# Seven products of the last feed-forward block: one more PSUM bank for each group, the evictions of two corners joined, six banks in turn instead of four

## The chip, the cores and the metric

The kernel runs on one core of a Trainium2 chip (trn2). The metric is the device time of one execution in microseconds (us), as the median of several runs. The core's engines run side by side and meet only at semaphores: TensorE (PE) multiplies and adds up in PSUM, which has eight banks of 512 float32 per partition; VectorE (DVE) and ScalarE (ACT) read PSUM and work in SBUF; SyncE (SP) issues the transfers. Each engine works through its own list of instructions in order, so an instruction that waits holds back all that stand behind it on that engine.

## The reference

The reference is one inference step of a decoder trunk with two layers, in float32. Each layer has a token mixer (an mLSTM in the first, gated linear attention in the second) and then a dense SwiGLU feed-forward, each between two RMS norms and added to x:

```
def swiglu(x, w_gate, w_up, w_down):
    h = jax.nn.silu(einsum('bsd,df->bsf', x, w_gate)) * einsum('bsd,df->bsf', x, w_up)
    return einsum('bsf,fd->bsd', h, w_down)

for i in range(DEPTH):
    mix, state = mixer_i(rms_norm(x, g_pre_mix[i]), ...)
    x = x + rms_norm(mix, g_post_mix[i])
    x = x + rms_norm(swiglu(rms_norm(x, g_pre_ffn[i]), w_ffn_gate[i], w_ffn_up[i], w_ffn_down[i]), g_post_ffn[i])
```

There are 1024 prompt tokens and 64 sample tokens, the model is 1024 wide, the feed-forward 2816 wide (22 tiles of 128).

## The kernel before

**Units.** The 1088 tokens are worked in block 0 (512 tokens) and block 1 (576 tokens, as two halves of 288 since a PSUM bank takes 512). `Plan` (from L118) writes a list of units, one per weight tile of 128x1024: P (input projection), W (output projection), G (gate), U (up), D (down; four output tiles for a pair of hidden tiles). Every engine's program walks this list. A float32 weight tile is split in a high part (`w_hi`, ACT, L1618) and a low part (`w_lo`, DVE, L2061), and each product is three matmuls: low x high, high x high, high x low. Weight tiles live in rings of three: `hi(n)` waits until unit n-3 has finished its matmuls (semaphore `groups`), `lo(n)` waits for `hi(n)`, and the transfer of a tile waits for `lo` of three units before.

**Seven products.** In block 1 of the second layer's feed-forward, the last large stage of the kernel, 18 groups (9 of gate, 9 of up, in turn) compute two neighbouring tiles at once. Two tiles x two halves of the contraction x two halves of the tokens would be eight products of 12 matmuls; with sums of weights (S1, S2, S4) and of inputs (T0 to T3) it is seven. A group is two units, first and second. In TensorE's order (`seven_first`, L1255; `seven_second`, L1276) with banks X, Y, Z:

1. product 1 into X; 2. product 2 (S2) into Y; 3. product 3 (S1) into Z; 4. product 4 added to Y;
5. product 5 added to X, which is corner c11; 6. product 6 (second tile x T3) into Y anew; 7. product 7 (S4) added to Z.

ScalarE copies X after product 1 (L1648, `first_copy`). VectorE forms U2 = Y + copy after product 2, U3 = Y + copy after product 4, c22 = Z + U3 at once, then c21 = Y + U3 after product 6 and c12 = Z + U2 after product 7 (all L2105). Product 6 waits for U3, since it overwrites Y, and product 7 waits for c22, since it adds to Z. For a gate group ScalarE then puts c11 through silu (L1654, `first_silu`, which waits for product 5), splits a weight tile (`hi`, L1618), and puts c21 and c22 together through silu (L1659); c12 follows (L1664). For an up group VectorE multiplies c11 (L2129) and in `gate` the three others (L2145) with the gate's values.

**Order on VectorE.** In the second unit of a gate group it is: U3, c22, `lo(n + 2)`, c21; then, in eight of the gate groups, a piece of block 0's last norm (`post`, L2340 and L2343). In the D unit that follows it is c12, the weight sums of the next group (`s3_s2`, L2084 and L2087), and the evictions Y of the four down tiles (L2202), with splits between them.

**Banks.** `Plan.banks` hands out banks 0 to 3 in turn; block 1's tiles take two at a time, so in a D unit tile q waits until tile q-2 (or what was there before) is evicted. Banks 4 to 7 (`M0` = 4) belong to mixers and norms; in this stage the norm of block 0 uses banks 4 and 5.

**Start of the stage.** The sums T0 to T3 are formed on VectorE (`tsum`) and split (`tq`, L1703 and L2236) while the last down units of block 0 (D, L2297) run. The order of the units is G0, D, D, U0, G1, U1, then the first group of seven. G, U with a number are hidden tiles of block 1 that are computed in the ordinary way.

Of the kernel before, what the change touches and what calls it, by code (L numbers as in the profile page):

```python
# [13 lines left out]
P = 128  # L14
# [94 lines left out]
class Plan:  # L109
# [61 lines left out]
    def banks(self):  # L171
        at, n = 0, 0
        counts = {"act": 0, "dve": 0}
        held = [None] * 4
        for u in self.units:
            if u.seven:
                z = u.seven
                if not u.second:
                    z.banks = [(at + c) % 4 for c in range(3)]
                    z.vacated = [dict([held[b]]) for b in z.banks]  # L180
                    at = (at + 3) % 4
                    z.t1 = counts["act"] = counts["act"] + 1
                    z.u2 = counts["dve"] = counts["dve"] + 1
                else:
                    order = ("u3", "c22", "c21", "c12") if z.kind == "G" else ("u3", "c22", "c11", "c21", "c12")
                    if z.kind == "G":
                        z.c11 = counts["act"] = counts["act"] + 1
                    ev = {}
                    for name in order:
                        counts["dve"] += 1  # L190
                        ev[name] = counts["dve"]
                    z.u3, z.c22, z.c21, z.c12 = ev["u3"], ev["c22"], ev["c21"], ev["c12"]
# [3 lines left out]
                    held[z.banks[1]] = ("dve", z.c21)  # L196
                    held[z.banks[2]] = ("dve", z.c12)
                u.groups.append(Group(n, z.banks[u.second], {}, 0))
                n += 1
                continue  # L200
            by = "dve" if u.kind in "UD" or u.late else "act"
            if u.part is not None:
                if u.part == 0:
                    mine = [Group(0, (at + c) % 4, {held[(at + c) % 4][0]: held[(at + c) % 4][1]}, 0) for c in range(4)]
                if u.part < 3:
                    u.groups.append(Group(n, None, {}, 0))
                    n += 1
                for c, grp in enumerate(mine if u.part == 3 else ()):
                    counts[by] += 1
                    grp.n, grp.ev = n, counts[by]  # L210
                    held[grp.bank] = (by, grp.ev)
                    u.groups.append(grp)
                    n += 1
                u.chunks = mine
                continue
            for _ in range(4 if u.kind == "D" else 1):
                if u.blk and at % 2:
                    at = (at + 1) % 4
                mine = range(at, at + NG[u.blk])
# [5 lines left out]
                u.groups.append(Group(n, at, vacated, counts[by]))  # L225
                for b in mine:
                    held[b] = (by, counts[by])
                at = (at + NG[u.blk]) % 4
                n += 1
# [10 lines left out]
def schedule(plan):  # L240
# [254 lines left out]
def memory(nc, ctx):  # L495
# [31 lines left out]
    g.E = sb("evicted", [P, 3, NT[1]])  # L527
    g.C = sb("state", [P, H, DV + 1])
# [45 lines left out]
    g.UC = piece("n", "up_corner", [P, GW[1]])  # L574
# [68 lines left out]
def program(nc, g, plan, a):  # L643
# [114 lines left out]
    n_gated = 0  # L758
    for n, u in enumerate(units):
        if u.seven and not u.second:  # L760
            sevens[n] = u.seven
            u.seven.n, u.seven.hid0, u.seven.gated0 = n, u.hid0, n_gated
            n_gated += 3 * (u.kind == "U")
# [22 lines left out]
    n = 0  # L786
# [29 lines left out]
    with nc.Block() as block:  # L816
# [288 lines left out]
        def _(pe):  # L1105
# [149 lines left out]
            def seven_first(z):  # L1255

                a, b = z.n % NW, (z.n + 1) % NW
                X, Y, Z = z.banks
# [3 lines left out]
                half_product(g.whi[:, a, 0:512], g.wlo[:, a, 0:512], quarter(HH, 0, 0), quarter(HL, 0, 0), X).then_inc(s["prod"], 1)  # L1262
# [6 lines left out]
                vacant(z.vacated[2])  # L1269
# [6 lines left out]
            def seven_second(z):  # L1276

                a, b = z.n % NW, (z.n + 1) % NW
                X, Y, Z = z.banks
                HH, HL = g.HH[1], g.HL[1]  # L1280
                pe.wait_ge(s["left_act"], z.t1)
# [318 lines left out]
        def _(act):  # L1600
# [26 lines left out]
            def s2_s1_high(z):  # L1627
                act.wait_ge(s["sums"], 4 * z.g + 2)
                wait(act, s["prod"], 5 * (z.g - 1) + 2)
                act.activation(g.S2H[:, :], g.SF[:, :], ACT.Copy).then_inc(s["s_hi"], 1)  # L1630
                act.wait_ge(s["sums"], 4 * z.g + 3)
                wait(act, s["prod"], 5 * (z.g - 1) + 3)
                act.activation(g.S1H[:, :], g.S1[:, :], ACT.Copy).then_inc(s["s_hi"], 1)

            def s4_high(z):
                act.wait_ge(s["sums"], 4 * z.g + 4)
                wait(act, s["prod"], 5 * z.g)
                act.activation(g.S4H[:, :], g.SF[:, :], ACT.Copy).then_inc(s["s_hi"], 1)

            def first_copy(z):  # L1640

                act.wait_ge(s["prod"], 5 * z.g + 1)
                act.wait_ge(s["hid_lo_ready"], z.hid0 - 2 * (z.kind == "G" and z.g > 0))
                if z.kind == "U":
                    act.wait_ge(s["left_dve"], z.mate.c21)
                elif z.g:
                    act.wait_ge(s["gated"], z.gated0 - 1)
# [9 lines left out]
            def second_silu(z):  # L1657
                act.wait_ge(s["left_dve"], z.c21)
# [8 lines left out]
            def hid_high(z):  # L1667
                for j, c in enumerate((1, 0)):
                    act.wait_ge(s["left_dve"], z.c11)
                    act.wait_ge(s["gated"], z.gated0 + 2 + j)  # L1670
                    act.activation(g.hh[:, c, :], g.E[:, c, :], ACT.Copy).then_inc(s["hid_hi_ready"], 1)

            def seven_unit(n, u):

                z, before, after = u.seven, ended(n), sevens.get(n + 1)
                if not u.second:
# [3 lines left out]
                    if before:  # L1680
                        hid_high(before)
# [8 lines left out]
                hi(n + 2)  # L1690

            def between(n):

                before = ended(n)
                if before:
                    third_silu(before) if before.kind == "G" else hid_high(before)
# [8 lines left out]
            def evict(u):  # L1705
# [46 lines left out]
                elif u.kind == "G":  # L1752
# [6 lines left out]
                    if u.i < 2:  # L1759
                        wait(act, s["hid_lo_ready"], u.hid0 - u.i)  # L1760
# [267 lines left out]
            for n, u in enumerate(units):  # L2028
# [16 lines left out]
                evict(u)  # L2045
                if n + 1 in sevens:
                    s2_s1_high(sevens[n + 1])
                for t in u.tags:
# [4 lines left out]
        def _(dve):  # L2053
# [35 lines left out]
            def s1_sum(z):  # L2089
                summed(z, 2)  # L2090
                wait(dve, s["prod"], 5 * (z.g - 1) + 3)
# [15 lines left out]
            def u2_sum(z):  # L2107
                dve.wait_ge(s["prod"], 5 * z.g + 2)
# [7 lines left out]
            def u3_c22(z):  # L2116
                dve.wait_ge(s["prod"], 5 * z.g + 4)
                add_to(U3(), z.banks[1], U3())
                dve.wait_ge(s["left_dve"], z.u3)
# [3 lines left out]
                add_to(g.E[:, 1, GW[1]:] if z.kind == "G" else g.UC[:, :], z.banks[2], U3())  # L2123
# [7 lines left out]
            def c21(z):  # L2131
                dve.wait_ge(s["groups"], units[z.n + 1].groups[0].n + 1)
                add_to(g.E[:, 1, 0:GW[1]] if z.kind == "G" else U3(), z.banks[1], U3())

            def c12(z):
                dve.wait_ge(s["prod"], 5 * z.g + 5)
                add_to(g.E[:, 0, GW[1]:] if z.kind == "G" else U2(), z.banks[2], U2())

            def gate(z):

                for E, up, silu, left in ((g.E[:, 1, GW[1]:], g.UC[:, :], 1, z.c22), (g.E[:, 1, 0:GW[1]], U3(), 1, z.c21),
                                          (g.E[:, 0, GW[1]:], U2(), 2, z.c12)):
                    dve.wait_ge(s["silu"], z.mate.g + silu)
                    dve.wait_ge(s["left_dve"], left)
                    dve.tensor_tensor(E, up, E, ALU.mult).then_inc(s["gated"], 1)  # L2145
# [8 lines left out]
            def seven_first(n, z, before):  # L2154

                if before:
                    c12(before)
                    if before.kind == "U":
                        gate(before)
# [10 lines left out]
            def seven_second(n, z, after):  # L2170
# [628 lines left out]
            for n, u in enumerate(units):  # L2799
# [15 lines left out]
                if before:  # L2815
                    c12(before)
                    gate(before)
# [18 lines left out]
                seven_ahead(n)  # L2836
# [101 lines left out]
```

## Time and profile before

| | |
|---|---|
| median of 3 runs | 2555.53 us (2555.3 to 2555.64) |
| the profiled execution's own time | 2555.54 us |
| its span in the trace | 2553.5 us |
| granted TensorE clock, mean | 0.999 |
| PE busy | 2533.4 us (99%) |
| DVE busy | 1622.4 us (64%) |
| ACT busy | 1056.4 us (41%) |
| stage of the seven products | about 2156 to 2482 us of the span, a period of 35.8 us |

A period is one gate group, two D units and one up group: 84 + 96 + 84 = 264 matmuls. A matmul's recorded duration (about 295 ns) is longer than the distance to the next one (about 132 ns), because they overlap; so a wait of TensorE is read from the starts of its weight loads (PEld), which come one per matmul. Times below are microseconds from the span's start.

### The profile page before, as it was taken

What the parts mean: (1) busy time and instruction counts of PE and PEld (TensorE: products, weight loads), DVE (VectorE), ACT (ScalarE), POOL (GpSimd) and SP (SyncE); (2) the same over time, 40 slices, a digit from 0 to 9 for tenths busy, and PEclk for the clock granted to TensorE, in tenths of its full rate; (3) what the DMA queues carried; (4) which work ended last, traced back from release to release, by engine and by line L of the source; (5) the groups of instructions that cost most, each with busy time, mean ns of one, the idle gap of its engine ahead of it and who ended that gap; (6) DMA issues with size and microseconds to landing.
All of it is one profiled execution on the core that took longest, in us unless ns stands there. A gap on an engine that the chain in (4) does not pass through costs nothing.

```text
span 2553.5 us, 40896 instructions
## 1 busy us (share of the span) xinstructions
PE 2533.4 (99%) x16985; PEld 2287.3 (90%) x16985; DVE 1622.4 (64%) x2562; ACT 1056.4 (41%) x1537; POOL 0.2 (0%) x4
## 2 busy tenths in 40 slices
PE   9999999999999999999999999999999999999998
PEld 7899898887988998889998988998887988999998
DVE  6743575566467673357754776327877388888875
ACT  5443355442334442444524344326453345333332
POOL 0000000000000000000000000000000000000000
PEclk9999999999999999999999999999999999999999
DMA  6454445435433433543323343344436333333332
GB/s 227 136 181 154 144 152 158 143 113 167 153 114 106 137 103 97 164 156 99 110 94 126 96 146 111 134 146 135 133 89 215 121 128 105 102 97 91 104 97 93
DMA packets 176707, 330.40 MB, mean 129 GB/s; under 512 B 19964, under 2 KB 93436, under 8 KB 176524
## 3 DMA queue, kind: packets, MB, share of 16 engines
q1 hardware_dynamic: 176524, 327.79, 40.4%
q8 instruction: 135, 2.21, 0.4%
q14 instruction: 48, 0.39, 0.0%
HBM read 271.46 MB, written 56.28 MB: 128 GB/s over the span
## 4 chain that ended last, share of the span: by engine, by line
PE 89%; DVE 6%; ACT 2%; issue 1%; DMA 1%; SPq 0%; DVEq 0%; ACTq 0%
PE ps L1118 71%; PE ps L1246 6%; PE ps L1132 3%; PE ps L1496 1%; DVE w_lo L2061 1%; ACT w_hi L1618 1%; PE ps L1438 1%; PE ps L1582 1%; DVE Y L2297 1%; PE ps L1427 1%; PE ps L1421 1%; DVE Y L2340 0%; PE ps L1300 0%; PE ps L1150 0%; PE ps L1420 0%
## 5 line engine op out<-in xcount | busy, mean ns | idle before, releaser
L1118 PE MATMUL ps<-HH,w_lo 128*128 128x288 f32 (+1 forms) x2904 | 968.4, 333 | 1.7 <-DVE Y L2297 1.6
L1118 PE MATMUL ps<-HL,w_hi 128*128 128x288 f32 (+1 forms) x2904 | 958.3, 330 | 0.0
L1118 PE MATMUL ps<-HH,w_hi 128*128 128x288 f32 (+1 forms) x2904 | 957.8, 330 | 0.0
L2061 DVE TENSOR_TENSOR w_lo<-w_stage,w_hi 128x1024 fp32r<-128x1024 f32 x392 | 478.3, 1220 | 231.8 <-ACT w_hi L1618 230.7
L1118 PEld LDWEIGHTS ps<-HH,w_lo 128*128 128x128 f32 x2904 | 544.9, 188 | 50.7 <-issue 6.0
L1118 PEld LDWEIGHTS ps<-HL,w_hi 128*128 128x128 f32 x2904 | 544.9, 188 | 43.0
L1118 PEld LDWEIGHTS ps<-HH,w_hi 128*128 128x128 f32 x2904 | 545.0, 188 | 41.6
L1618 ACT ACTIVATE w_hi<-w_stage 128x1024 fp32r<-128x1024 f32 x392 | 412.4, 1052 | 316.7 <-PE ps L1118 268.9
L1118 PE MATMUL ps<-hid_hi,w_lo 128*128 128x288 f32 (+1 forms) x1052 | 349.7, 332 | 5.3 <-DVE Y L2297 2.1
L1118 PE MATMUL ps<-hid_lo,w_hi 128*128 128x288 f32 (+1 forms) x1052 | 343.6, 327 | 0.0
L1118 PE MATMUL ps<-hid_hi,w_hi 128*128 128x288 f32 (+1 forms) x1052 | 343.4, 326 | 0.0
L2297 DVE TENSOR_TENSOR Y<-ps,Y 128x512 f32<-128x512 f32 (+1 forms) x255 | 178.5, 710 | 74.5 <-PE ps L1118 74.3
L1118 PEld LDWEIGHTS ps<-hid_hi,w_lo 128*128 128x128 f32 x1052 | 197.4, 188 | 28.4 <-issue 4.0
L1118 PEld LDWEIGHTS ps<-hid_lo,w_hi 128*128 128x128 f32 x1052 | 197.5, 188 | 14.0
L1118 PEld LDWEIGHTS ps<-hid_hi,w_hi 128*128 128x128 f32 x1052 | 197.5, 188 | 13.1
L1769 ACT ACTIVATE hid_hi<-evicted 128x512 fp32r<-128x512 f32 (+1 forms) x70 | 45.6, 651 | 256.3 <-DVE evicted L2279 256.3
L2072 DVE TENSOR_TENSOR n_sum<-n_sum,n_sq 128x512 f32<-128x512 f32 (+1 forms) x110 | 79.4, 721 | 92.7 <-ACT n_sq L1624 88.9
L1736 ACT ACTIVATE evicted<-ps 128x576 f32<-128x576 f32 (+1 forms) x64 | 40.8, 637 | 211.9 <-PE ps L1118 211.8
L2279 DVE TENSOR_TENSOR evicted<-ps,evicted 128x512 f32<-128x512 f32 (+1 forms) x70 | 49.9, 712 | 78.6 <-PE ps L1118 78.5
L1765 ACT ACTIVATE evicted<-ps 128x512 f32<-128x512 f32 (+1 forms) x70 | 43.1, 616 | 98.7 <-PE ps L1118 98.0
L2282 DVE TENSOR_TENSOR hid_lo<-evicted,hid_hi 128x512 fp32r<-128x512 f32 (+1 forms) x70 | 50.2, 717 | 50.2 <-ACT hid_hi L1769 50.2
L1624 ACT ACTIVATE n_sq<-n_xs 128x512 f32<-128x512 f32 (+1 forms) x64 | 41.7, 657 | 91.3 <-DVE n_xs L2343 84.4
(323 smaller groups left out, 2899.4 us busy)
## 6 DMA issues: line engine op xcount, KB each, us to landing
w_stage<-w_gate_in SPq DMA_DIRECT2D x88, 512.0 KB, 3.7
w_stage<-w_up_in SPq DMA_DIRECT2D x88, 512.0 KB, 3.6
w_stage<-w_down_in SPq DMA_DIRECT2D x88, 512.0 KB, 3.6
w_stage<-w_in_in SPq DMA_DIRECT2D x80, 512.0 KB, 3.8
w_stage<-w_out_in SPq DMA_DIRECT2D x32, 512.0 KB, 3.6
proj_scratch<-evicted SPq DMA_DIRECT2D x48, 288.0 KB, 2.2
proj_scratch<-evicted SPq DMA_DIRECT2D x32, 256.0 KB, 2.1
w_stage<-w_v_in SPq DMA_DIRECT2D x16, 512.0 KB, 4.1
```

What stands on the lines that cost most here:

```text
L1118: mm = pe.matmul(ps[:, grp.bank + t, 0:W], wsl(w, k), x[:, k, t * W:(t + 1) * W], start=(k == first and m == 0), stop=(k == last and m == 2))
L1132: mm = pe.matmul(ps[:, grp.bank, :], x[:, k, t], w[:, n % NW, cols], start=(k == 0 and m == 0), stop=(k == KD - 1 and m == 2))
L1246: mm = pe.matmul(ps[:, bank, 0:GW[1]], w[:, k * P:(k + 1) * P], x[:, k, :], start=start and k == 0 and m == 0, stop=k == KD // 2 - 1 and m ...
L1618: act.activation(g.whi[:, n % NW, :], g.wst[:, n % NW, :], ACT.Copy).then_inc(s["w_hi"], 1)
L1624: act.activation(grouped(dst, b) if src.shape != dst.shape else dst, src, ACT.Square).then_inc(s["squared"], 1)
L1765: act.activation(grouped(g.E[:, c, 0:NT[b]], b), bank(grp.bank, b), ACT.Silu).then_inc(s["left_act"], 1)
L1769: act.activation(g.hh[:, u.i % 2, 0:NT[b]], g.E[:, 2, 0:NT[b]], ACT.Copy).then_inc(s["hid_hi_ready"], 1)
L2061: dve.tensor_tensor(g.wlo[:, n % NW, :], g.wst[:, n % NW, :], g.whi[:, n % NW, :].bitcast(F32), ALU.subtract).then_inc(s["w_lo"], 1)
L2072: dve.tensor_tensor(acc, acc, sq, ALU.add).then_inc(s["summed"], 1)
L2279: dve.tensor_tensor(grouped(pr, b), bank(grp.bank, b), grouped(g.E[:, u.i % 2, 0:NT[b]], b), ALU.mult).then_inc(s["left_dve"], 1)
L2282: dve.tensor_tensor(g.hl[:, u.i % 2, 0:NT[b]], pr, g.hh[:, u.i % 2, 0:NT[b]].bitcast(F32), ALU.subtract).then_inc(s["hid_lo_ready"], 1)
L2297: dve.tensor_tensor(Y, bank(grp.bank, b), Y, ALU.add).then_inc(s["left_dve"], 1)
```

## The change

It does five things.

- In the last stage (from the first G of block 1 in layer 2) the banks in turn are six: 0, 1, 2, 3, 6, 7.
- A group of seven takes four of them: X, Y, W, Z, with W and Z side by side. Product 6 goes to W, starts anew there, and stands ahead of product 5. It no longer waits for U3, and its number is the fifth.
- VectorE forms c21 and c22 in one instruction of 576 columns, `c2`, from banks W and Z; product 7 waits for it, in place of c22. `c2` waits for product 6. In a gate group it stands behind `lo(n + 2)`; in an up group behind S2's split and S4's sum of the next group.
- `gate` is two instructions: c21 and c22 together, right behind `c2`, then c12. `hid_high` of that half moves to the second unit.
- At the start of the stage the order is G0, G1, D, D, U0, U1; `tq` 2 and 3, the load of x for block 0's norm (`xload` 8) and the weight sums ahead of the first group stand earlier.

```diff
-        self.puts(A1[49:-2] + B1[:1] + A1[-2:] + B1[1:])
+        self.puts(A1[49:-2] + B1[0:3:2] + A1[-2:] + B1[1:4:2] + B1[4:])
@@ Plan.banks
+            if u.layer == 1 and u.blk == 1 and u.kind == "G":
+                pool = (0, 1, 2, 3, 6, 7)
+            size = len(pool)
-                    z.banks = [(at + c) % 4 for c in range(3)]
+                    at = (at + at % 2) % size
+                    z.banks = [pool[(at + c) % size] for c in range(4)]
-                    order = ("u3", "c22", "c21", "c12") if z.kind == "G" else ("u3", "c22", "c11", "c21", "c12")
+                    order = ("u3", "c2", "c12") if z.kind == "G" else ("u3", "c2", "c11", "c12")
@@ schedule
-        tag(f + (0, 0, 3, 4)[i], "tq", i)
-    tag(f + 5, "xload", 8)
+        tag(f + i // 2, "tq", i)
+    tag(f + 3, "xload", 8)
@@ TensorE, seven_second
+                vacant(z.vacated[2])
+                half_product(g.whi[:, b, 512:1024], g.wlo[:, b, 512:1024], g.TH[:, 3], g.TL[:, 3], W
+                             ).then_inc(s["prod"], 1)
                 pe.wait_ge(s["left_act"], z.t1)
                 half_product(g.whi[:, a, 512:1024], g.wlo[:, a, 512:1024], quarter(HH, 1, 0), quarter(HL, 1, 0), X, False
-                             ).then_inc(s["groups"], 1)
-                pe.wait_ge(s["left_dve"], z.u3)
-                half_product(g.whi[:, b, 512:1024], g.wlo[:, b, 512:1024], g.TH[:, 3], g.TL[:, 3], Y
-                             ).then_inc(s["groups"], 1)
+                             ).then_inc(s["groups"], 2)
                 pe.wait_ge(s["s_lo"], 3 * z.g + 3)
-                pe.wait_ge(s["left_dve"], z.c22)
+                pe.wait_ge(s["left_dve"], z.c2)
                 half_product(g.S4H, g.S4L, quarter(HH, 1, 1), quarter(HL, 1, 1), Z, False).then_inc(s["prod"], 1)
@@ ScalarE, seven_unit (second unit; unchanged but for its last line)
                 if z.kind == "G":
                     first_silu(u)
                     hi(n + 2)
                     second_silu(z)
                     return
                 if after:
                     s2_s1_high(after)
                 hi(n + 2)
+                hid_high(z, 0)
@@ VectorE
+            def c2(z):
+                dve.wait_ge(s["prod"], 6 * z.g + 5)
+                dve.wait_ge(s["left_dve"], z.u3)
...
+                out = grouped(g.E[:, 1, :], 1) if z.kind == "G" else g.UC[:, :, :]
+                dve.tensor_tensor(out, bank(z.banks[2], 1), U3().unsqueeze(1).to_broadcast([P, 2, GW[1]]), ALU.add
+                                  ).then_inc(s["left_dve"], 1)
@@ VectorE, seven_second
-                u3_c22(z)
+                u3_sum(z)
+                if z.kind == "G":
+                    lo(n + 2)
+                    c2(z)
+                    return
                 if after:
                     s_low(after, 0)
-                if z.kind == "G":
-                    lo(n + 2)
-                    c21(z)
-                    return
+                    s4_sum(after)
+                c2(z)
+                gate(z, 0)
                 c11_product(z)
                 if after:
-                    s4_sum(after)
                     s_low(after, 1)
-                c21(z)
                 lo(n + 2)
@@ VectorE, main loop: the weight sums ahead of a group
                 if u.kind != "D" and n + 2 < len(units):
                     lo(n + 2)
+                seven_ahead(n)
...
-                seven_ahead(n)
```

## Rows read from the trace of the kernel before

**Rows 1.** The page: busy time of each engine, its share of the span, and instructions.
```profile
PE 2533.4 (99%) x16985; PEld 2287.3 (90%) x16985; DVE 1622.4 (64%) x2562; ACT 1056.4 (41%) x1537; POOL 0.2 (0%) x4
```

**Rows 2.** The chain of waits in time: start us, us, what; the groups of two periods.
```profile
2220.91 19.13 PE ps L1246 x144
...
2256.67 19.13 PE ps L1246 x144
```

**Rows 3.** Timeline of weight loads: start us, us, engine line op [idle before <-releaser].
```profile
2239.73 0.19 PEld L1246 LDWEIGHTS ps<-t_hi,w_lo 128*128 128x128 f32 x1
...
2241.32 0.19 PEld L1246 LDWEIGHTS ps<-HH,n_s_lo 128*128 128x128 f32 x1
...
2244.85 0.19 PEld L1118 LDWEIGHTS ps<-hid_hi,w_lo 128*128 128x128 f32 x1 [0.27 <-DVE evicted L2105]
...
2246.84 0.19 PEld L1118 LDWEIGHTS ps<-hid_hi,w_lo 128*128 128x128 f32 x1 [0.37 <-DVE Y L2202]
```

**Rows 4.** Who waited for whom, 2195 to 2475: us in total, times, longest.
```profile
DVE w_lo L2061 <- ACT w_hi L1618: 16.2, 8, 2.0
...
PEld ps L1118 <- DVE Y L2202: 3.0, 8, 0.4
PEld ps L1118 <- DVE evicted L2105: 2.2, 8, 0.3
```

**Rows 5.** Timeline of ScalarE, second unit of a gate group.
```profile
2240.06 0.41 ACT L1654 ACTIVATE evicted<-ps 128x288 f32<-128x288 f32 x1 [4.83 <-PE ps L1246]
2240.36 1.05 ACT L1618 ACTIVATE w_hi<-w_stage 128x1024 fp32r<-128x1024 f32 x1
```

**Rows 6.** Timeline of VectorE, the same gate group and the D units behind it.
```profile
2241.45 1.23 DVE L2061 TENSOR_TENSOR w_lo<-w_stage,w_hi 128x1024 fp32r<-128x1024 f32 x1 [2.02 <-ACT w_hi L1618]
2242.59 0.45 DVE L2105 TENSOR_TENSOR evicted<-ps,evicted 128x288 f32<-128x288 f32 x1
2242.96 0.74 DVE L2340 SCALAR_TENSOR_TENSOR Y<-Y,vec,n_rstd 128x512 f32<-128x512 f32 x1
...
2251.93 0.76 DVE L2202 TENSOR_TENSOR Y<-ps,Y 128x576 f32<-128x576 f32 x1 [0.24 <-PE ps L1118]
```

**Rows 7.** Timeline of VectorE, then of weight loads, second unit of an up group.
```profile
2227.55 0.45 DVE L2105 TENSOR_TENSOR evicted<-ps,evicted 128x288 f32<-128x288 f32 x1
2228.03 0.46 DVE L2105 TENSOR_TENSOR n_up_corner<-ps,evicted 128x288 f32<-128x288 f32 x1
2228.41 0.68 DVE L2102 TENSOR_TENSOR s_lo<-n_s_s,s_hi 128x512 fp32r<-128x512 f32 x1
...
2230.16 0.19 PEld L1246 LDWEIGHTS ps<-HH,n_s_lo 128*128 128x128 f32 x1
```

**Rows 8.** Start of the stage, timeline of weight loads: those that had waited.
```profile
2129.46 0.19 PEld L1118 LDWEIGHTS ps<-hid_hi,w_lo 128*128 128x128 f32 x1 [1.39 <-issue]
...
2137.06 0.19 PEld L1118 LDWEIGHTS ps<-HH,w_lo 128*128 128x128 f32 x1 [1.96 <-DVE w_lo L2061]
...
2160.74 0.19 PEld L1246 LDWEIGHTS ps<-t_hi,s_lo 128*128 128x128 f32 x1 [2.53 <-DVE s_lo L2102]
...
2175.32 0.19 PEld L1118 LDWEIGHTS ps<-hid_hi,w_lo 128*128 128x128 f32 x1 [1.45 <-DVE Y L2200]
```

**Rows 9.** The same stretch: busy us (instructions) of PE, PEld, DVE, ACT; then timelines.
```profile
2130.00:2160.00 30.00, 26.85 (x181) 24.93 (x179) 24.44 (x33) 17.52 (x23) 0.00 (x0) 1.00 0.18 54
...
2163.49 0.46 DVE L2105 TENSOR_TENSOR evicted<-ps,evicted 128x288 f32<-128x288 f32 x1 [0.62 <-ACT evicted L1648]
...
2149.88 1.28 ACT L1765 ACT_TABLE_LOAD   x1
```

**Rows 10.** TensorE's last matmuls; windows: length, PE busy, granted clock, DMA share, GB/s.
```profile
2541.78 4.04 PE L1352 MATMUL ps<-Y,ident 128*128 128x288 f32 x16
...
2548.00:2548.50 0.50, 0.00 (x0) 0.94 0.98 378
2548.50:2549.00 0.50, 0.00 (x0) 0.50 1.00 373
```

More of the change, by code:

```diff
@@ L178, in banks @@
                 if not u.second:
-                    z.banks = [(at + c) % 4 for c in range(3)]
-                    z.vacated = [dict([held[b]]) for b in z.banks]
-                    at = (at + 3) % 4
+                    at = (at + at % 2) % size
+                    z.banks = [pool[(at + c) % size] for c in range(4)]
+                    z.vacated = [dict([held[b]] if held[b] else []) for b in z.banks]
+                    at = (at + 4) % size
                     z.t1 = counts["act"] = counts["act"] + 1
@@ L191, in banks @@
                         ev[name] = counts["dve"]
-                    z.u3, z.c22, z.c21, z.c12 = ev["u3"], ev["c22"], ev["c21"], ev["c12"]
+                    z.u3, z.c2, z.c12 = ev["u3"], ev["c2"], ev["c12"]
                     if z.kind == "U":
@@ L195, in banks @@
                     held[z.banks[0]] = ("act" if z.kind == "G" else "dve", z.c11)
-                    held[z.banks[1]] = ("dve", z.c21)
-                    held[z.banks[2]] = ("dve", z.c12)
+                    held[z.banks[1]] = ("dve", z.u3)
+                    held[z.banks[2]] = ("dve", z.c2)
+                    held[z.banks[3]] = ("dve", z.c12)
                 u.groups.append(Group(n, z.banks[u.second], {}, 0))
@@ L217, in banks @@
                 if u.blk and at % 2:
-                    at = (at + 1) % 4
-                mine = range(at, at + NG[u.blk])
+                    at = (at + 1) % size
+                mine = range(pool[at], pool[at] + NG[u.blk])
                 vacated = {}
@@ L224, in banks @@
                 counts[by] += 1
-                u.groups.append(Group(n, at, vacated, counts[by]))
+                u.groups.append(Group(n, pool[at], vacated, counts[by]))
                 for b in mine:
                     held[b] = (by, counts[by])
-                at = (at + NG[u.blk]) % 4
+                at = (at + NG[u.blk]) % size
                 n += 1
@@ L762, in program @@
             u.seven.n, u.seven.hid0, u.seven.gated0 = n, u.hid0, n_gated
-            n_gated += 3 * (u.kind == "U")
+            u.seven.before = last_seven
+            last_seven = u.seven
+            n_gated += 2 * (u.kind == "U")
     def ended(n):
@@ L1257, in seven_first @@
                 a, b = z.n % NW, (z.n + 1) % NW
-                X, Y, Z = z.banks
+                X, Y, W, Z = z.banks
                 HH, HL = g.HH[1], g.HL[1]
@@ L1636, in s4_high @@
                 act.wait_ge(s["sums"], 4 * z.g + 4)
-                wait(act, s["prod"], 5 * z.g)
+                wait(act, s["prod"], 6 * z.g)
                 act.activation(g.S4H[:, :], g.SF[:, :], ACT.Copy).then_inc(s["s_hi"], 1)
             def first_copy(z):
-                act.wait_ge(s["prod"], 5 * z.g + 1)
+                act.wait_ge(s["prod"], 6 * z.g + 1)
                 act.wait_ge(s["hid_lo_ready"], z.hid0 - 2 * (z.kind == "G" and z.g > 0))
[L1644 to L1647, printed above, removed]
+                if z.before:
+                    act.wait_ge(s["left_dve"], z.before.c2)
                 act.activation(U3(), ps[:, z.banks[0], 0:GW[1]], ACT.Copy).then_inc(s["left_act"], 1)
@@ L1680, in seven_unit @@
                     if before:
-                        hid_high(before)
+                        hid_high(before, 1)
                     return
@@ L1695, in between @@
                 if before:
-                    third_silu(before) if before.kind == "G" else hid_high(before)
+                    third_silu(before) if before.kind == "G" else hid_high(before, 1)
             def t_half(i):
@@ L1759, in evict @@
                     if u.i < 2:
-                        wait(act, s["hid_lo_ready"], u.hid0 - u.i)
+                        wait(act, s["hid_lo_ready"], u.hid0 - (u.i if units[n - 1].kind == "U" else 0))
                     elif unit("U", u.layer, b, u.i - 2).seven:
@@ L2090, in s1_sum @@
                 summed(z, 2)
-                wait(dve, s["prod"], 5 * (z.g - 1) + 3)
+                wait(dve, s["prod"], 6 * (z.g - 1) + 3)
                 dve.tensor_tensor(g.S1[:, :], g.SF[:, :], stage(z.n, 0), ALU.add).then_inc(s["sums"], 1)
@@ L2129, in c11_product, with gate @@
                 dve.tensor_tensor(E, ps[:, z.banks[0], 0:GW[1]], E, ALU.mult).then_inc(s["left_dve"], 1)
-            def c21(z):
-                dve.wait_ge(s["groups"], units[z.n + 1].groups[0].n + 1)
-                add_to(g.E[:, 1, 0:GW[1]] if z.kind == "G" else U3(), z.banks[1], U3())
             def c12(z):
[L2136 to L2145, printed above, removed]
+                dve.wait_ge(s["prod"], 6 * z.g + 6)
+                add_to(g.E[:, 0, GW[1]:] if z.kind == "G" else U2(), z.banks[3], U2())
+            def gate(z, j):
+                dve.wait_ge(s["silu"], z.mate.g + 1 + j)
+                dve.wait_ge(s["left_dve"], z.c12 if j else z.c2)
+                if j:
+                    dve.tensor_tensor(g.E[:, 0, GW[1]:], U2(), g.E[:, 0, GW[1]:], ALU.mult).then_inc(s["gated"], 1)
+                else:
+                    dve.tensor_tensor(grouped(g.E[:, 1, :], 1), g.UC[:, :, :], grouped(g.E[:, 1, :], 1), ALU.mult
+                                      ).then_inc(s["gated"], 1)
             def hid_low(z, j):
@@ L2158, in seven_first @@
                     if before.kind == "U":
-                        gate(before)
+                        gate(before, 1)
                 s_low(z, 2)
@@ L2816, in _ @@
                     c12(before)
-                    gate(before)
+                    gate(before, 1)
                     hid_low(before, 0)
```

39 lines of the change are left out of this document (20 added, 19 removed).

## Prediction

> **What bounds the kernel now.** I read the page first: TensorE is busy 99% of the span, VectorE 64%, ScalarE 41% [rows 1]. So time goes or comes only where TensorE's row of matmuls opens or closes. Then the chain of waits in time, which shows how regular the last stage is: from one pair of groups to the next it is 2256.67 - 2220.91 = 35.76 us [rows 2]. Then the weight loads one by one, as matmul records overlap: the twelve of product 6 take 2241.32 - 2239.73 = 1.59 us, 0.1325 each [rows 3], and 264 of them 34.98 us. The rest of a period, 0.78 us, is two waits in the D unit behind the gate group. A load lasts 0.19 and loads come 0.13 apart, so a wait costs TensorE the idle time shown plus 0.06: 0.27 + 0.06 = 0.33 for the bank that c12 still holds, and 0.37 + 0.06 = 0.43 for the first down tile's eviction [rows 3]; each is there eight times [rows 4]. At the start of the stage there are larger ones (matmuls of 512 columns come 0.23 apart, so there the idle time counts less 0.04): 1.35 and 1.92 in and behind block 0's last D units, 2.59 before product 2 of the first group, 1.51 in the first D unit of block 1 [rows 8]. All that more banks could win in this stage is thus 8 x 0.76 + 7.4 = 13.5 us, 0.5% of the time. (0.2%, 5.1 us, is about what a measurement of this kernel can tell from no change.)
>
> **Gate groups: a new wait ahead of product 7.** This decides the sign. Before, c22 was read ahead of `lo`, so product 7 was free long before its turn. Now product 7 waits for `c2`, and on VectorE `c2` stands behind `lo(n + 2)`. That waits for `hi(n + 2)` on ScalarE, which stands behind `first_silu`; both wait for product 5, the one right ahead of product 7 in TensorE's order. So TensorE finishes product 5 and then sits through a whole chain over ScalarE and VectorE. VectorE's wait is in the trace already, with no harm yet: it idles 2.02 us before `lo`, eight times, 16.2 us [rows 4, 6]. The links, from the end of product 5, whose successor's first load starts at 2239.73:
> - to the silu: 2240.06 - 2239.73 = 0.33 [rows 3, 5];
> - silu to `hi`: 2240.36 - 2240.06 = 0.30 [rows 5];
> - `hi` to `lo`: 2241.45 - 2240.36 = 1.09 [rows 5, 6];
> - `lo` to the next VectorE instruction: 2242.59 - 2241.45 = 1.14 [rows 6];
> - `c2` itself: the trace has no sum from two banks with one operand read twice. The nearest row is the addition of 576 columns out of PSUM, 0.76 [rows 6]; below it is one corner, 0.45, and above two corners, 0.92 [rows 6, 7]. I take 0.76;
> - from VectorE to TensorE 0.05: the weight load of 2246.84 follows an eviction at about that distance.
>
> Sum 3.67 us, between 3.4 and 3.8, in each of nine gate groups: +33.0 us. Behind the waiting product 7 on TensorE stand the D units and all that follows; nothing covers it. In the first group the silu table has to be loaded too: the norm's exp comes after G1 now, so the load of 1.28 us that G1's silu paid [rows 9] falls to `first_silu`: +1.3.
>
> **D units: both waits go, -6.1 us.** With six banks a down tile waits for the one three before it, 4.8 us away. c12 sits in bank 3, which only the third tile takes. The piece of the norm, which starts at 2242.96 [rows 6] and made the first eviction late, now runs while TensorE waits for nothing else than `c2`; it stands behind `c2`, so it doesn't lengthen the wait. 8 x 0.76 = 6.1. The first D unit's 1.51 was VectorE waiting for a weight tile that landed late; the load of x that shared the DMA engines with it is now issued earlier, and the longer group covers the rest: -1.5.
>
> **Up groups: nothing.** VectorE's order is U3, split of S2, sum S4, `c2`. From 2227.55: U3 0.38, split and sum at most 0.68 each, so `c2` starts by 2229.3 and ends by 2230.05, plus 0.05. Product 7's turn is 2230.16 [rows 7]. Product 6, for which `c2` waits, ends at 2228.57 + 0.3. I take 0, for 0.1 us of slack; if it is late by a whole split, 0.6 in each of nine, +5. It can't gain, since nothing waited here. Fewer instructions on VectorE (one for two corners, two for three in `gate`) save about 0.3 a period where it idles anyway: 0.
>
> **Start of the stage: nothing.** G1's 48 matmuls now cover the splits of T, and the down tiles have six banks, so 1.35 and 1.92 at block 0's D units go. But VectorE is the one that is late here: it is busy 24.44 of 30 us [rows 9], its work stays the same, and two more splits of T (1.3 each) come ahead of the first down eviction. Carrying its list forward in the new order (D's evictions and norm sums from about 2133.6 for 12 us, the norm's reciprocal root, U0, U1, the sums for the first group), I get U2 of the first group at about 2163.5, where it is now: 2163.49 [rows 9]. TensorE waits in other places (rstd, product 2, product 4) for the same sum. I take 0; at best all three go, 1.35 + 1.92 + 2.59 = 5.9 gained; at worst 2 lost.
>
> **The clock.** It is granted at 1.00, that is 2.4 GHz, over the stage. It fell to 0.50 (1.2 GHz) once in this trace, close to 2548.0 to 2548.5, about 2.6 us after TensorE's last matmul ended at 2545.82 [rows 10]; the idle stretch of 2.53 before product 2 [rows 8] did not bring it down. The new wait leaves TensorE idle for about 3.5 us, longer than both. No row here shows matmuls at the lower level. At half the clock a product takes 1.59 more, so a fall costs about that, with 0 and 9 falls as the ends: 0 to 14.3. I take two falls, +3.2.
>
> The Trainium skill (TensorE: Matmul & The Clock Gate, section "HAM oscillation — how this bites in real kernels") says that gaps between bursts of matmuls can send the clock down again and again, each burst starting cold. By it all nine waits would pay, and the sum would be 11 us higher; the second rival is that. This trace shows one fall, after the last matmul, which agrees, and none in a shorter gap.
>
> **Sum.** Against the profiled execution's own 2555.54 (span 2553.5 and 2.0 around it; the median of the runs is 2555.53, so no shift): + 33.0 + 1.3 - 6.1 - 1.5 + 3.2 = +29.9, 2585.4; I say 2585 us.
>
> **Rivals.**
> 1. The waits in the D units stay: they would be VectorE's lateness and not the banks'. The second wait's releaser is an eviction that stood behind the norm piece. Against it: VectorE gets that piece done in the new wait. 2585 + 7.6 = 2593.
> 2. The clock falls in every gate group and stays down for one to two products: 2585 - 3.2 + 14.3 = 2596, up to 2610. For it: the idle time is longer than that after which it fell; against: only one such case.
> 3. The start gains in full: 2585 - 5.9 = 2579. For it: banks were waited for there; against: VectorE's 24.44 of 30.
> 4. The other side, faster: product 7 does not wait for `lo`. If the high part of that tile were ready before product 5 ends, `c2` would be done in time and only the gains stay: 2555.5 - 6.1 - 1.5 = 2548. It decides at the moment when `hi` starts: before the end of product 5 or behind it. For it speaks only that `c2`'s other inputs are early; against it, that ScalarE's `hi` starts 0.30 behind a silu that waits for product 5 [rows 5], in all eight periods [rows 4].
> 5. The change doesn't do what it says, by halves: the down units still take banks that groups hold. Product 7's wait is as computed, the gain 3 less: 2588, inside the forecast.
>
> **How the numbers follow.** Forecast (with 5) 0.66, own range 2575 to 2594; rival 1 0.08; rival 2 0.12; rival 3 0.08; rival 4 0.06. Low: the start's gain and no fall of the clock, 2579 - 3.2, less 3 for a shorter `c2`: 2573. High: 2600, which takes in rival 1 and the lower part of rival 2. Faster 0.06, within 0.2% 0.02, slower 0.92.
>
> **What would show it.** In the timeline of weight loads each gate group has a gap of about 3.7 us before product 7, released by a VectorE addition of 576 columns of some 0.76; the chain of waits shows L1618 and L2061 in each period; the period is 35.76 - 0.76 + 3.67 = 38.7 us. VectorE's idle time before `lo` in the gate group becomes some 4.0 (2.02, one product of 1.59, and c22's 0.4), with `c2` right behind. No load in the D units waits. The granted clock in windows of a few us shows the falls. It would be wrong if product 7 of the gate groups follows product 5 without a gap, if up groups wait too, or if the start of the stage moves product 1 of the first group by more than 3 us against product 4.

## The result: 1.45% slower, as forecast in sign and cause

| | before | after |
|---|---|---|
| median of four runs | 2555.47 us | 2593.51 us |
| fastest and slowest | 2555.30, 2555.64 | 2590.90, 2594.91 |
| profiled execution | 2555.54 | 2593.95 |
| its span, mean granted clock | 2553.5, 0.999 | 2592.2, 0.993 |

The ratio is 1.0145 (95% interval 1.0133 to 1.0157). The forecast was 2585, with 2573 to 2600 as its range: 8.5 us short. Of the runs in this document three executions stand apart and stay unexplained: one each of experiments 1 and 6 took over 6000 us at clock 1.00 (without them these two medians would be 0.15 and 0.2 lower), and one of experiment 9 took 2549.89 at 0.948. Line numbers of the kernel after are some ten higher (L1618 is now L1628, L2061 is L2070).

**The profile after.** The page's busy times, and the chain that ended last by engine, against [rows 1]:

```profile
PE 2543.1 (98%) x16985; PEld 2301.2 (89%) x16985; DVE 1621.8 (63%) x2535; ACT 1056.1 (41%) x1537; POOL 0.2 (0%) x4
PE 92%; DVE 5%; ACT 2%; issue 2%; DVEq 0%; ACTq 0%
```

VectorE and ScalarE are no busier, and their shares of the chain are no larger either (before it was PE 89%, DVE 6%, ACT 2%). What has changed is where they stand in it. The chain of waits in order of time (start, length, engine, line; "issue" is time without a wait that the profile shows) tells where, in one period, against [rows 2]:

```profile
2228.18 20.71 PE ps L1255 x156
2248.89 0.02 issue
2248.91 0.02 ACT evicted L1662
2248.94 0.28 issue
2249.22 1.06 ACT w_hi L1628
2250.28 0.02 issue
2250.30 0.04 DVE w_lo L2070
2250.34 0.05 issue
2250.38 0.05 DVEq L490
2250.43 1.01 issue
2251.44 0.76 DVE evicted L2137
2252.20 0.14 issue
2252.34 2.70 PE ps L1255 x12
```

This is the predicted chain link by link: product 5 ends, `first_silu` at 2248.91, `hi` at 2249.22, `lo` at 2250.30, `c2` at 2251.44 for 0.76, and product 7. The waits grouped by who waits for whom (total, times, longest), first TensorE's from 2150 to 2525 us:

```profile
PE ps L1255 <- DVE evicted L2137: 31.2, 9, 3.5
PE ps L1255 <- DVE s_lo L2111: 2.8, 1, 2.8
PE ps L1255 <- DVE evicted L2114: 1.7, 1, 1.7
```

L2137 is `c2`, nine times. The other two are the start of the stage. No weight load in a D unit waits any more, where there had been sixteen [rows 4]. VectorE's own wait for `hi`, 2195 to 2510 us, was 16.2 in eight [rows 4]:

```profile
DVE w_lo L2070 <- ACT w_hi L1628: 32.9, 8, 4.1
```

The weight loads of the same group one by one (start, us, tiles, in brackets the idle time ahead of it and its releaser), the last of product 5 and the first of product 7, against [rows 3]:

```profile
2248.46 0.19 PEld L1255 LDWEIGHTS ps<-HL,w_hi 128*128 128x128 f32 x1
2252.31 0.19 PEld L1255 LDWEIGHTS ps<-HH,n_s_lo 128*128 128x128 f32 x1 [3.66 <-issue]
```

From load to load 3.85 us, where 0.13 would be without a wait: 3.72 lost, and so in all nine groups. On VectorE, against [rows 6]:

```profile
2250.30 1.23 DVE L2070 TENSOR_TENSOR w_lo<-w_stage,w_hi 128x1024 fp32r<-128x1024 f32 x1 [4.11 <-ACT w_hi L1628]
2251.44 0.75 DVE L2137 TENSOR_TENSOR evicted<-ps,evicted 128x576 f32<-128x576 f32 x1
2252.11 0.74 DVE L2354 SCALAR_TENSOR_TENSOR Y<-Y,vec,n_rstd 128x512 f32<-128x512 f32 x1
```

The norm piece stands behind `c2` and under the cover of product 7. What the forecast had too small is in the table of stretches (stretch, its length, PE busy with instructions, granted clock, DMA share, GB/s), one stretch a period:

```profile
2168.50:2209.70 41.20, 37.74 (x266) 0.92 0.25 77
2209.70:2248.50 38.80, 35.34 (x267) 1.00 0.30 89
2248.50:2288.70 40.20, 36.74 (x265) 0.96 0.27 86
2288.70:2329.00 40.30, 36.84 (x266) 0.96 0.29 86
2329.00:2370.20 41.20, 37.74 (x267) 0.92 0.28 84
2370.20:2408.90 38.70, 35.24 (x266) 1.00 0.28 89
2408.90:2449.20 40.30, 36.84 (x266) 0.96 0.27 86
2449.20:2489.50 40.30, 36.84 (x267) 0.96 0.29 85
2489.50:2530.70 41.20, 37.74 (x267) 0.92 0.29 84
```

The two periods at 1.00 last 38.75, the forecast's 38.7. Seven are longer: four at 0.96 by 1.5 us, three at 0.92 by 2.45. The same view in small steps around one wait:

```profile
2248.50:2252.70 4.20, 0.74 (x6) 1.00 0.00 0
2252.70:2253.20 0.50, 0.50 (x6) 0.77 0.00 0
2253.20:2256.00 2.80, 2.80 (x13) 0.50 0.47 162
2256.00:2256.50 0.50, 0.50 (x4) 0.61 0.67 238
```

Here the clock holds 1.00 through the idle time, falls to 0.50 (1.2 GHz) as the matmuls resume, and is back at 1.00 from about 2256.4 on. At 0.50 weight loads come 0.24 us apart instead of 0.1325; these two are five apart:

```profile
2254.60 0.33 PEld L1127 LDWEIGHTS ps<-hid_hi,w_lo 128*128 128x128 f32 x1
2255.80 0.33 PEld L1127 LDWEIGHTS ps<-hid_lo,w_hi 128*128 128x128 f32 x1
```

So 1 us of matmuls at 0.50 costs 1 - 0.1325 / 0.24 = 0.45 us, and the 3.4 us from 2253.0 to 2256.4 cost the 1.5 us of this period. In the three periods at 0.92 the clock falls earlier, while TensorE still waits. In the first of them product 7's first load comes at 2172.36, and the granted clock was already

```profile
2171.00:2171.50 0.50, 0.00 (x0) 0.55 0.00 0
```

and 0.50 from there to about 2177.9. That leaves 5.5 us of matmuls at 0.50, which cost the 2.45.

### The profile page after: what moved, and what is told of

It reads as the page before. It is cut to its first block, busy times and chain, and to the rows that moved or that the text cites. A ratio compares the mean times of both kernels' runs of the same rounds, so it can differ in the third digit from the quotient of the medians.

```text
span 2592.2 us, 40859 instructions
## 1 busy us (share of the span) xinstructions
PE 2543.1 (98%) x16985; PEld 2301.2 (89%) x16985; DVE 1621.8 (63%) x2535; ACT 1056.1 (41%) x1537; POOL 0.2 (0%) x4
## 4 chain that ended last, share of the span: by engine, by line
PE 92%; DVE 5%; ACT 2%; issue 2%; DVEq 0%; ACTq 0%
PE ps L1127 71%; PE ps L1255 8%; PE ps L1141 3%; PE ps L1506 1%; ACT w_hi L1628 1%; PE ps L1159 1%; PE ps L1448 1%; PE ps L1592 1%; DVE Y L2311 1%; PE ps L1437 1%; PE ps L1431 1%; PE ps L1310 0%; DVE w_lo L2070 0%; PE ps L1430 0%; PE ps L1539 0%
## 5 line engine op out<-in xcount | busy, mean ns | idle before, releaser
L2070 DVE TENSOR_TENSOR w_lo<-w_stage,w_hi 128x1024 fp32r<-128x1024 f32 x392 | 478.5, 1221 | 249.7 <-ACT w_hi L1628 248.7
L1628 ACT ACTIVATE w_hi<-w_stage 128x1024 fp32r<-128x1024 f32 x392 | 412.1, 1052 | 335.9 <-PE ps L1127 278.4
```

What stands on the lines that cost most here:

```text
L1628: act.activation(g.whi[:, n % NW, :], g.wst[:, n % NW, :], ACT.Copy).then_inc(s["w_hi"], 1)
L2070: dve.tensor_tensor(g.wlo[:, n % NW, :], g.wst[:, n % NW, :], g.whi[:, n % NW, :].bitcast(F32), ALU.subtract).then_inc(s["w_lo"], 1)
```

## The experiments

The "kernel before" was timed again beside each (its median there is given). Theory: product 7 waits because `c2` stands behind `lo(n + 2)`, which waits for a tile whose high part starts only after product 5; the clock adds to it. Rivals: contention for banks, or the order at the start of the stage.

**1. `c2` ahead of `lo`**, nothing else changed.

```diff
                 if z.kind == "G":
-                    lo(n + 2)
                     c2(z)
+                    lo(n + 2)
                     return
```

> The changed kernel with c2 ahead of lo(n + 2) in the gate groups. Theory (VectorE's order makes the wait ahead of product 7, and the clock falls because of it): the nine gaps of 3.72 us go (33.5 us) and the clock stays at 1.00 (13.4 us), so about 2547 us if no wait comes back in the D units. I expect one to come back: lo and the piece of the norm are then late again, the first down tile is evicted until about 0.4 us after the fourth one wants its bank, so 0.4 a period against 0.76 before the change: 2550 us. Rival (the gaps come from the four banks or from c2's width, not from lo): 2590 us or more, gaps stay.

Measured: 2551.16 us against 2556.65, ratio 0.9978 (0.9969 to 0.9987). The gap ahead of product 7 is gone from all nine groups, and the mean clock is 0.999. One line moved takes back the whole 38 us and 5.5 more. The waits of weight loads in 2195 to 2475 us, and one of them:

```profile
PEld ps L1127 <- DVE Y L2216: 2.5, 8, 0.3
```
```profile
2247.24 0.19 PEld L1127 LDWEIGHTS ps<-hid_hi,w_lo 128*128 128x128 f32 x1 [0.31 <-DVE Y L2216]
```

The first D wait (the bank c12 held) stays away, the second is back at 0.31 + 0.06 = 0.37, since `lo` and the norm piece again run late.

**2. The wait filled with matmuls.** To price the clock, the kernel after gets 26 extra matmuls behind product 5 of each gate group, into two banks that nothing reads; their results are not used.

```diff
                              ).then_inc(s["groups"], 2)
+                if z.kind == "G":
+                    for i in range(26):
+                        pe.matmul(ps[:, M0 + i % 2, 0:GW[1]], HH[:, 0, 0:P], g.TH[:, 3, i % 4, :], start=True, stop=True)
```

> The changed kernel with 26 extra matmuls (3.4 us, results unused) behind product 5 of each gate group, where TensorE waits. Theory (7 of 9 waits bring the clock down, which costs 13.4 us beyond the waits): the clock stays at 1.00 in the stage, the load of product 7 starts when it did, 2593.5 - 13.4 = 2580 us. Rival (the 13.4 us are something else in these periods): 2593 us or more.

Measured: 2581.01 us against 2556.65, 1.0096 (1.0082 to 1.0110): 12.5 us less than the kernel after, with 234 matmuls more. The table of stretches, in two that hold all nine groups (their ends are not those of this kernel's periods):

```profile
2168.50:2209.70 41.20, 41.12 (x311) 1.00 0.26 78
2209.70:2530.00 320.30, 319.62 (x2399) 1.00 0.30 92
```

The chain over ScalarE and VectorE is as long as before (in the first group product 7's first load comes 8.48 us behind product 4's, 8.47 in the kernel after), only the clock does not fall in the groups. From the first gate tile's first load to the first load of the last product 7 it is 2507.05 - 2117.03 = 390.02 us here and 2519.62 - 2116.35 = 403.27 in the kernel after: 13.25 less, where the table of the kernel after gives 4 x 1.5 + 3 x 2.45 = 13.4. (The spans differ by 2592.2 - 2579.6 = 12.6, since this execution came to the stage 0.7 later.) So of the 38 us some 13 are the clock's. The other 25 are the waits of 33.5 less what the D units and the start give back.

One fall there is in this trace, ahead of the groups, at the wait before product 2 of the first group, 2.8 us long as in the kernel after, where the clock stayed up:

```profile
2160.00:2162.00 2.00, 2.00 (x11) 0.50 0.26 55
```

It costs nothing: product 4, which waits for VectorE in any case, comes 47.53 us after the first gate tile's first load, and 47.54 in the kernel after.

**3. The kernel before with its corner late**: four banks, three-bank groups, but c22 behind `lo(n + 2)` in gate groups.

```diff
                 add_to(U3(), z.banks[1], U3())
+                if z.kind == "U":
+                    c22(z)
+
+            def c22(z):
                 dve.wait_ge(s["left_dve"], z.u3)
...
                     lo(n + 2)
+                    c22(z)
                     c21(z)
```

> The kernel before with one edit: c22 of the gate groups behind lo(n + 2). Theory (the order on VectorE alone is enough): product 7 waits for the chain less product 6, which still covers 1.6 us: about 1.84 us in each of nine groups; the D units' waits of 0.76 and the first one of 1.5 go in exchange: 2564 us, clock 1.00. Rival (banks, c2 or product order are needed for the loss): 2555.5 us, no gap ahead of product 7.

Measured: 2565.38 us against 2556.65, 1.0035 (1.0021 to 1.0049). TensorE's waits from 2150 to 2530 us, and a first load of the product that waits:

```profile
PE ps L1246 <- DVE evicted L2105: 14.1, 9, 1.6
```
```profile
2245.36 0.19 PEld L1246 LDWEIGHTS ps<-HH,n_s_lo 128*128 128x128 f32 x1 [1.78 <-issue]
```

Nine gaps of 1.97 - 0.13 = 1.84 us, half the length, since product 6 still covers 1.6 us of the chain and c22 alone takes 0.3 less than `c2`; 16.6 us lost, 7.6 won at the D units, whose waits are gone with four banks too: +9.0, measured +8.7. The order on VectorE alone makes the wait, and with TensorE's waits at 1.6 us the clock stays at 1.00.

**4. Experiment 1 with four banks.**

```diff
-                pool = (0, 1, 2, 3, 6, 7)
+                pool = (0, 1, 2, 3)
```

> e1 with four banks in turn instead of six. Theory (with groups of four banks, six in turn are needed): the second down tile waits for c12, about 1.5 us, the third for the first's eviction, 0.5: some 1.6 a period more than e1, 2563 us. Rival (the waits in the D units are VectorE's lateness, whatever the banks): as e1 within 2 us.

Measured: 2564.53 us against 2556.65, 1.0032 (1.0019 to 1.0044). The waits of weight loads, 2195 to 2470 us:

```profile
PEld ps L1127 <- DVE evicted L2114: 12.1, 8, 1.5
PEld ps L1127 <- DVE Y L2216: 2.5, 7, 0.4
```

A group of four banks in a pool of four makes the D unit wait for c12 for 1.5 us instead of the 0.27 of [rows 3]. So the two extra banks are needed for the four-bank group, and are worth 13.4 us to it; that is a price which the change itself brought in.

**5. The start of the stage as before** (experiment 1 with the old unit order and the old places of T's splits and of the load of x; the weight sums stay early).

```diff
-        self.puts(A1[49:-2] + B1[0:3:2] + A1[-2:] + B1[1:4:2] + B1[4:])
+        self.puts(A1[49:-2] + B1[:1] + A1[-2:] + B1[1:])
...
-        tag(f + i // 2, "tq", i)
-    tag(f + 3, "xload", 8)
+        tag(f + (0, 0, 3, 4)[i], "tq", i)
+    tag(f + 5, "xload", 8)
```

> e1 with the old start of the stage: the order G0, D, D, U0, G1, U1, and tq 2, 3 and xload 8 where they were; the early weight sums stay. Theory (VectorE's list bounds the start, so its new order gave nothing; only the earlier load of x takes away the 1.5 in the first D unit): 1.5 to 2 slower than e1, 2553 us. Rival (the new start won the 5.9 of its three waits): 2557 us.

Measured: 2549.17 us against 2556.16, 0.9973 (0.9962 to 0.9984). Both expectations missed: undoing the order made it faster. The measure of the start is the time from the first gate tile's first load to that of product 4 of the first group. The two loads in this kernel:

```profile
2117.62 0.19 PEld L1127 LDWEIGHTS ps<-HH,w_lo 128*128 128x128 f32 x1 [0.60 <-DVE w_lo L2070]
2163.60 0.19 PEld L1255 LDWEIGHTS ps<-t_hi,w_lo 128*128 128x128 f32 x1 [1.95 <-issue]
```

and in the kernel after:

```profile
2116.35 0.19 PEld L1127 LDWEIGHTS ps<-HH,w_lo 128*128 128x128 f32 x1 [0.55 <-DVE w_lo L2070]
2163.89 0.19 PEld L1255 LDWEIGHTS ps<-t_hi,w_lo 128*128 128x128 f32 x1 [1.95 <-issue]
```

That is 47.54 us after (47.54 in experiment 1 too, 47.72 before), and 45.98 here. The near-zero of the start was two parts of opposite sign: the new order, with the places of the splits, costs 1.56, and what else moved there wins 47.72 - 45.98 = 1.74. What is left over is `seven_ahead`, called ahead of the tags, the high parts of these weight sums, which ScalarE now forms ahead of its own evictions, and the six banks. None of them was run alone. Experiment 4 speaks against the banks: with four of them product 4 comes at 2164.68 - 2117.14 = 47.54 us too.

**6. The norm piece between `c2` and `lo`** in gate groups, on top of experiment 1.

```diff
                     c2(z)
+                    for t in units[n].tags:
+                        if t[0] == "post":
+                            post(*t[1:])
                     lo(n + 2)
...
-                        if t[0] in steps:
+                        if t[0] in steps and t[0] != "post":
```

> e1 with the piece of the norm between c2 and lo(n + 2), where VectorE waits for ScalarE anyway. Theory (the wait of 0.37 that e1 has left in each period is the first down tile's eviction, late by the piece of the norm): all eight go, 2551.2 - 3.0 = 2548.2 us. Rival (that eviction is late for the weight sums or lo itself): as e1.

Measured: 2548.21 us against 2556.16, 0.9969 (0.9956 to 0.9981). No weight load waits from 2195 to 2470 us. The second D wait was the norm piece standing ahead of the first eviction; VectorE was idle ahead of `lo` and could take it there.

**7. The reciprocal root of the last norm later**, on top of 6: into the first up group, where it had stood ahead of the first group's U sums.

```diff
-    ffn_norm(3, 0, u + 1, [(at["G", 1, 1, 2 * p + 1, 0] - u - 1, 1) for p in range(2, 10)])
+    v = at["U", 1, 1, 3, 0]
+    ffn_norm(3, 0, v, [(at["G", 1, 1, 2 * p + 1, 0] - v, 1) for p in range(2, 10)])
```

> e6 with the reciprocal root of block 0's norm moved from U0 into the second unit of the first up group of seven. Theory (with VectorE's list the bound at the start, the root's chain over ScalarE and its three instructions are what makes products 2 and 4 of the first group late): of the start's 6.0 us of waits some 3.5 go, 1.5 come back where the root now stands, 2546 us. Rival (the start waits for the splits of T and the weight sums alone): as e6, or 1 to 2 slower.

Measured: 2545.57 us against 2556.16, 0.9958 (0.9945 to 0.9970). Product 4 comes 42.27 us after the first load, 5.3 sooner; where the root stands now, two waits of 0.74 and 1.77 from load to load give 2.3 back. In the kernel after, VectorE's list has the root's three instructions there, and a wait of 1.9 for what ScalarE does for it:

```profile
2154.05 0.69 DVE L2338 SCALAR_TENSOR_TENSOR n_sum<-n_rstd 128x512 f32<-128x512 f32 x1 [1.91 <-ACT n_rstd L1805]
```

The three take 2156.23 - 2154.05 = 2.2 us, so 4.1 of the 5.3 are these, and the rest stands ahead of them, at the root's partial sums. That bears out that VectorE's list, with its waits for ScalarE in it, bounds the start; and the 47.54 of experiment 4 says that it isn't the banks.

**8. `hi` ahead of `first_silu`** in gate groups of the kernel after: the shortest chain with `lo` still ahead of `c2`.

```diff
                 if z.kind == "G":
-                    first_silu(u)
                     hi(n + 2)
+                    first_silu(u)
```

> The changed kernel with hi(n + 2) ahead of first_silu in the gate groups. Theory (the gap ahead of product 7 is the sum of its links): the silu's link of 0.30 goes, the gap is 3.42 instead of 3.72 in nine groups, 2.7 us less; the clock falls as often or less, 2585 to 2591 us. Rival (hi would have to wait for something else at that point, the transfer of its tile): gap and time as in the changed kernel.

Measured: 2589.93 us (2584.94 to 2593.99) against 2556.16, 1.0126 (1.0110 to 1.0141). TensorE's waits and a first load of product 7:

```profile
PE ps L1255 <- DVE evicted L2137: 29.0, 9, 3.2
```
```profile
2252.74 0.28 PEld L1255 LDWEIGHTS ps<-HH,n_s_lo 128*128 128x128 f32 x1 [3.42 <-issue]
```

The gap is 3.61 - 0.13 = 3.48, 0.24 less (0.30 had been expected), which is the silu's place: 2.2 us in nine. The clock took that back in the profiled execution (2593.66, mean clock 0.991; it fell in seven of nine periods, four of them at 0.92, as this one) and not in another (2584.94, 0.997).

```profile
2290.20:2331.30 41.10, 37.88 (x267) 0.92 0.29 84
```

The runs differ by 9 us, in the same kernel, and the clock goes along with the time. A shorter chain by way of ScalarE wins too little to matter while `lo` stands ahead of `c2`.

**9. Experiment 7 with the old start of experiment 5.**

> e7 with the old order of the start (G0, D, D, U0, G1, U1, and tq 2, 3 and xload 8 where they were). In e5 the old order brought product 4 of the first group 1.6 us forward. If that is the order's own (the splits of T stand behind the down units' evictions, not ahead of them), it adds to e7: 2544 us. Rival (it only overlapped with the root's chain, which e7 has moved away, and what is left then is G1 and its silu): as e7 or slower, 2546 to 2548 us.

Measured: 2544.72 us against 2556.48, 0.9959 (0.9945 to 0.9972). Product 4 comes at 41.15, another 1.1 sooner, but the total can't be told from that of experiment 7. Experiments 7 and 9 beat both kernels: some 0.4% faster than before, 1.8% faster than after.

## Why the prediction was right, and where its terms were off

| term | forecast | measured |
|---|---|---|
| wait ahead of product 7 | 9 x 3.67 = +33.0 | 9 x 3.72 = +33.5 |
| silu table load | +1.3 | 0 |
| waits in D units | -6.1 | -6.1 |
| first D unit | -1.5 | -1.75 |
| up groups | 0 | 0 |
| start | 0 | -0.2 |
| clock | +3.2 | +13.4 |
| tail and rounding | | -0.5 |
| sum | +29.9 | +38.4 (spans: +38.7) |

**The wait** was right by link, place and size, and experiments 1 and 3 show its cause: move one instruction and it is gone, do the same in the kernel before and it appears. Rival 4 (no wait) fell with it, for the reason given: `hi` starts only behind the silu.

**The D units.** Right in what goes. The reason was mixed, as experiments 1, 3, 4 and 6 show: the first wait goes with the extra banks once c12 stands in the fourth, the second goes when the norm piece runs earlier, which is VectorE's order and has nothing to do with banks. In the kernel after the new wait alone would hide both, as it does with four banks in experiment 3. Rival 1 (they stay) fell, though its 2593 is the number that was measured: that it is so near is luck.

**The first D unit.** The size was near; the 0.23 more are a second, small wait of that unit (at 2170.65 in the kernel before), which the forecast left out. But half of the reason is not borne out: in experiment 5 the load of x stands where it stood before, and that unit has no wait either. What covers the tile there was not isolated.

**Up groups** had 0.1 us of slack in the forecast, and none of them waits: L2137 stands nine times in TensorE's waits, once for each gate group. The slack is as thin as computed. `c2` on VectorE and product 7's first load on TensorE:

```profile
2236.59 0.75 DVE L2137 TENSOR_TENSOR up_corners<-ps,evicted 128x576 f32<-128x576 f32 x1
```
```profile
2237.46 0.19 PEld L1255 LDWEIGHTS ps<-HH,n_s_lo 128*128 128x128 f32 x1
```

It ends at 2237.34, 0.12 ahead of that load.

**The table load** was a wrong step: +1.3 forecast, 0 measured. I took it to run when `first_silu` comes up, behind its wait for product 5. On ScalarE of the kernel after it is an instruction of its own, which ran before:

```profile
2163.23 1.28 ACT L1662 ACT_TABLE_LOAD   x1
```

The first group's product 4 starts only at 2163.89, so the load is over (2164.51) well before product 5 ends.

**The clock** is the mis-sized term: two falls taken, seven happened, and three of them cost 2.45 and not the 1.6 of one product at half speed, since the clock stayed down for more matmuls than one product has. That was rival 2's mechanism at its price of 14.3, with 0.12 as its chance; its total of 2596 against 2593.5 measured. Experiment 2 shows it: with the same wait but TensorE occupied, the median falls by 12.5 us and the stage by 13.3. The rule of the Trainium skill (TensorE: Matmul & The Clock Gate, section "HAM oscillation — how this bites in real kernels") had it nearly right, falls in each gap between bursts; the trace has seven in nine. I had weighed one row, the fall at the end of the kernel, and shaded it by its being only one. It showed a fall 2.6 us after the last matmul, and the new idle time was 3.5; against it stood only an idle time of 2.5 without a fall. One row can't give a rate, but two of nine had no row behind it at all. So the forecast was right by the wait, and its range held the measured time because it left room for more falls; 2593.5 is at the very end of the inner range of 2575 to 2594.

**The start.** The sum was right at 0 and its account was not: two parts of 1.6 and 1.7 cancel (experiment 5). The claim that VectorE is what is late there held: TensorE's waits moved, 0.84 ahead of the norm's own matmuls, 3.05 ahead of product 2 and 1.95 ahead of product 4, for nearly the same time at product 4, and taking the root and its wait for ScalarE out of VectorE's list ahead of it (experiment 7) brought product 4 forward by 5.3.

## What to carry to other kernels

When a product is merged so that its last reader comes later, look what stands ahead of that reader on its own engine: an instruction that waits on data for two units ahead is harmless until something urgent is queued behind it. Price an idle stretch of TensorE by its length and by the clock that follows it, and if the trace holds one fall after a shorter stretch, count on a fall in most of the longer ones, not in all: in these traces 17 of 23 waits of 2.8 us or more. A fall costs only where TensorE's matmuls are what the time hangs on. A term of zero made of a gain and a loss is worth a run of each part: here the better half was to be had alone.

## What the runs showed of the hardware

- A wait of TensorE of 3.5 us brought the clock from 1.00 to 0.50 in seven of nine cases, at a price of 1.5 or 2.45 us; after two equal waits (from about 2210.1 and 2370.6 us) it did not fall. With waits of 3.2 us (experiment 8) it fell in seven of nine too, with waits of 1.6 (experiment 3) in none. What decides between fall and none among equal waits stays open.
- The wait of 2.8 us ahead of product 2 of the first group is the same in five traces. The clock fell there in experiments 2, 6 and 8 and stayed up in the kernel after and in experiment 1, and product 4 came 47.53 or 47.54 us after the first gate tile's first load in all five.
- At a granted clock of 0.50 the matmuls of 288 columns came 0.24 us apart, at 1.00 0.1325. The price of a fall is the time that matmuls ran at 0.50, times 0.45: 3.4 us in the four cheap ones, some 5.4 us in the three dear ones.
- Such falls make a kernel's time scatter: 4 us over four runs after, 9 us in experiment 8 (2584.94 at a mean clock of 0.997, 2593.99 at 0.991), against 0.9 at most in experiments 2 and 3, where it stays up in the groups.
- The load of ScalarE's table ran while the activation that needs it was still waiting, so 1.28 us cost nothing here.
